# Sparse attention (NSA) on one core: row maxima from a single-pass score matmul, exponentials taken from key-major scores and fed straight to the value product, heads unrolled

## The reference

```python
def masked_softmax(s, mask):
    s = jnp.where(mask, s, -jnp.inf)
    m = jnp.max(s, axis=-1, keepdims=True)
    m = jnp.where(jnp.isfinite(m), m, 0.0)
    p = jnp.exp(s - m)
    return p / jnp.maximum(jnp.sum(p, axis=-1, keepdims=True), 1e-30)

# per block of 128 queries, in nsa_mixer
sc = jnp.einsum('bkgqd,bkcd->bkgqc', qn, k_cmp).astype(jnp.float32) * scale
p_cmp = masked_softmax(sc, cmp_end[None, :] <= t[:, None])
o_cmp = jnp.einsum('bkgqc,bkcd->bkgqd', p_cmp.astype(v_cmp.dtype), v_cmp)
...
ss = jnp.einsum('bkgqd,bkqnd->bkgqn', qr, ks).astype(jnp.float32) * scale
p_s = masked_softmax(ss, (kpos <= t[:, None])[:, :, None])
o_slc = jnp.einsum('bkgqn,bkqnd->bkgqd', p_s.astype(vs.dtype), vs)
...
sw = jnp.einsum('bkgqd,bknd->bkgqn', qr, kw).astype(jnp.float32) * scale
p_w = masked_softmax(sw, wband & (start - SLIDE_WINDOW + ki >= 0))
o_win = jnp.einsum('bkgqn,bknd->bkgqd', p_w.astype(vw.dtype), vw)
o = gb[0][..., None] * o_cmp + gb[1][..., None] * o_slc + gb[2][..., None] * o_win
```

## Time and profile before

| | us |
|---|---|
| median of 3 runs | 4932.07 |
| lowest, highest | 4921.65, 4937.89 |
| the profiled execution, its own time | 4938.08 |
| its span | 4936.3 |
| first to last matmul of this stage | 369.2 (2173.2 to 2542.4) |

### The profile page before, as it was taken

The page is one execution under the profiler, slowest core; times in us unless marked ns, Lnnn a source line. Parts: engine busy times, 40 slices in busy tenths (PEclk is TensorE's granted clock), DMA queues, the critical chain, the costliest instruction groups (busy, mean ns, idle before and its releaser), DMA issues. The chain is left out here.

```text
span 4936.3 us, 63184 instructions
## 1 busy us (share of the span) xinstructions
PE 4619.3 (94%) x21804; PEld 3854.2 (78%) x21804; DVE 2554.3 (52%) x4786; ACT 1741.3 (35%) x2558; POOL 283.3 (6%) x390
## 2 busy tenths in 40 slices
PE   7999989988999899979899999479999999999999
PEld 6887777777888788778788887168888888888887
DVE  6534655654652663355543325859965542344444
ACT  2222233343222322234443223423366662322222
POOL 1100000000100010011100000000000000011010
PEclk9999999999999899965579999789999999999999
DMA  6522201202542453210012221023344444555553
GB/s 234 216 100 100 93 27 47 85 26 77 213 161 86 153 209 127 81 38 1 1 52 86 96 100 69 9 74 115 124 171 175 178 185 176 183 194 193 191 195 141
DMA packets 105432, 589.79 MB, mean 119 GB/s; under 512 B 11778, under 2 KB 12992, under 8 KB 59712
## 3 DMA queue, kind: packets, MB, share of 16 engines
q1 hardware_dynamic: 52800, 369.76, 21.0%
q0 software_dynamic: 52480, 218.13, 12.0%
HBM read 513.36 MB, written 74.48 MB: 119 GB/s over the span
## 5 line engine op out<-in xcount | busy, mean ns | idle before, releaser
L112 DVE TENSOR_TENSOR w_lo<-raw,w_hi 128x2048 fp32r<-128x2048 f32 x331 | 758.7, 2292 | 1160.3 <-ACT w_hi L104 1150.9
L124 PE MATMUL ps<-x_hi,w_hi 128*128 128x512 f32 x2896 | 1150.6, 397 | 43.1 <-DVE x_lo L364 19.8
L125 PE MATMUL ps<-x_lo,w_hi 128*128 128x512 f32 x2896 | 1136.8, 393 | 0.0
L126 PE MATMUL ps<-x_hi,w_lo 128*128 128x512 f32 x2896 | 1136.4, 392 | 0.0
L104 ACT ACTIVATE w_hi<-raw 128x2048 fp32r<-128x2048 f32 x331 | 632.6, 1911 | 815.1 <-PE ps L126 439.0
L124 PEld LDWEIGHTS ps<-x_hi,w_hi 128*128 128x128 f32 x2896 | 549.7, 190 | 162.2 <-issue 44.3
L126 PEld LDWEIGHTS ps<-x_hi,w_lo 128*128 128x128 f32 x2896 | 548.7, 189 | 116.1
L125 PEld LDWEIGHTS ps<-x_lo,w_hi 128*128 128x128 f32 x2896 | 549.9, 190 | 109.8
L2041 PE MATMUL ps<-w_hi,px_gh 128*128 128x512 f32 x1024 | 399.0, 390 | 0.0
L2041 PE MATMUL ps<-w_hi,px_gl 128*128 128x512 f32 x1024 | 399.0, 390 | 0.0
L2041 PE MATMUL ps<-w_lo,px_gh 128*128 128x512 f32 x1024 | 399.0, 390 | 0.0
(11 more groups left out here) (345 smaller groups left out, 6132.3 us busy)
## 6 DMA issues: line engine op xcount, KB each, us to landing
raw<-in_slabs SPq DMA_DIRECT2D x331, 1024.0 KB, 4.8
ada_ring<-in_w_ada POOLq DMA_DIRECT2D x160, 512.0 KB, 4.8
act_dram<-px_act POOLq DMA_DIRECT2D x64, 512.0 KB, 2.9
gate_dram<-ps_g POOLq DMA_DIRECT2D x16, 2048.0 KB, 7.3
px_g<-gate_dram POOLq DMA_DIRECT2D x32, 1024.0 KB, 7.8
px_ai<-act_dram POOLq DMA_DIRECT2D x64, 512.0 KB, 4.7
h_dram<-h SPq DMA_DIRECT2D x2, 2048.0 KB, 8.4
h<-h_dram SPq DMA_DIRECT2D x2, 2048.0 KB, 8.0
```

The source lines that it names most:

```text
L112: nc.vector.tensor_tensor(k.wlo[:, c % 2, :], k.raw[:, c % 2, :], k.whi[:, c % 2, :].bitcast(F32), ALU.subtract).then_inc(k.raw_free, 1)
L124: mm(out, hi, rhs_hi, start=start, stop=False)
L125: mm(out, hi, rhs_lo, start=False, stop=False)
L126: return mm(out, lo, rhs_hi, start=False, stop=stop)
```

## The change

The stage is written anew and its loop is unrolled over 16 heads. A head now has nine items `j`: 0 is the compressed branch, 1 to 4 and 5 to 8 are the selected and the window branch.

- **By query** (`by_query`, for the maxima only): the scores are computed query by row as before, but with the high part of the keys alone, one matmul instead of two. DVE masks and takes the maximum; what it writes besides (`na_junk`) is thrown away. One DVE instruction per head clamps and negates the 12 maxima of each query (`na_nm`).
- **Rows** (`rows`): four small transposes per head turn the negated maxima into three rows of 512 (`na_mrow`), copied from PSUM by ACT.
- **By key** (`by_key`): the scores are computed a second time, key by row, with keys as the stationary operand and up to 512 query columns moving, both parts. Into the same PSUM bank go a matmul of three rows (`na_pick` by `na_mrow`), which subtracts the maxima, and one with the identity and the diagonal mask (`na_diag`), or for the compressed branch one of 31 rows with its mask (`na_cmpT`).
- ACT takes the exponential straight from PSUM into `na_pt`, which is the stationary operand of the value product. The transposes of the probabilities, their copies, the bias and the row sums go away. The values get a column of ones (`na_vo`, `na_vco`, 65 columns), so that the row sum comes out of the value product.
- **Output**: once per head instead of once per block, 12 sums and 768 products at a time; two pairs of banks take turns.
- By query runs two heads ahead of the rest: for heads 0 and 1 it stands before everything else, and the last two heads have none beside them. Staging by GpSimd waits for the last by-key item of the head four before.

The core of the diff:

```diff
+            def by_query(h, j):
+                u = 9 * h + j
+                if j == 0:
+                    pe.wait_ge(s["staged"], h + 1)
+                if u > 1:
+                    pe.wait_ge(s["maxed"], u - 1)
...
+                    last = nc.tensor.matmul(bank(k, u % 2, n), qs[:, h % 4, 1, b * P:(b + 1) * P], kk[:, 0, at:at + n],
+                                            start=True, stop=True)
+            def by_key(h, j):
+                q = item(h, j)
+                pe.wait_ge(s["act"], max(q - 1, row_item(h) + 1))
+                if j == 0:
+                    out = k.ps[0:NC, (2 + q % 2) * T:(3 + q % 2) * T]
+                    nc.tensor.matmul(out, ident[0:NC, 0:NC], cmp_t[:], start=True, stop=False)
+                    for part in range(2):
+                        nc.tensor.matmul(out, kc[:, part, 32 * kv_of(h):32 * kv_of(h) + NC], qs[:, h % 4, 0, :],
+                                         start=False, stop=False)
+                    last = nc.tensor.matmul(out, pick[:, 0, 0:NC], mrow[:, h % 2, :], start=False, stop=True)
+                else:
...
+                    for part in range(2):
+                        nc.tensor.matmul(bank(k, 2 + q % 2, n), kk[:, part, at:at + P], qs[:, h % 4, 1, kb * P:T],
+                                         start=part == 0, stop=False)
+                    nc.tensor.matmul(bank(k, 2 + q % 2, n), pick[:, 1 + (j - 1) // 4, :], mrow[:, h % 2, kb * P:T],
+                                     start=False, stop=False)
+                    last = nc.tensor.matmul(bank(k, 2 + q % 2, P), ident[:], diag[:], start=False, stop=True)
...
-                scores(0)
-                scores(1)
-                for u in range(U):
-                    if u < U - 2:
-                        scores(u + 2)
-                    transposes(u)
-                    if u > 0:
-                        values(u - 1)
-                values(U - 1)
+            for h in range(2):
+                for j in range(9):
+                    by_query(h, j)
+            rows(0)
+            pe.wait_ge(s["consts"], 1)
+            pe.wait_ge(s["vo"], 1)
+            by_key(0, 0)
+            for h in range(NH):
+                for j in range(9):
+                    if j == 2 and h < NH - 1:
+                        rows(h + 1)
+                    if j < 8:
+                        by_key(h, j + 1)
+                    elif h < NH - 1:
+                        by_key(h + 1, 0)
+                    if h < NH - 2:
+                        by_query(h + 2, j)
+                    values(h, j)
```

More of the change, by code:

```diff
@@ L1249, in stage_attend_nsa @@
     nc = k.nc
-    NC, U = 31, 4 * NB * 3
+    NC, W = 31, HD + 1
     with ExitStack() as ctx:
@@ L1275, in blocks, with kv_of, keys_at, item @@
-        def blocks(n):
-            return [(j * P, min(P, n - j * P)) for j in range((n + P - 1) // P)]
+        def kv_of(h):
+            return h // 8
+        def keys_at(h, j):
+            return (2 * ((j - 1) // 4) + kv_of(h)) * T, (j - 1) % 4
+        def item(h, j):
+            return 1 + 10 * h + j + (j > 2 and h < NH - 1)
+        def row_item(h):
+            return 10 * h - 6 if h else 0
+        def out_at(h, b, i):
+            return bank(k, 4 + 2 * (h % 2) + b // 2, W, (3 * (b % 2) + i) * W)
@@ L1278, in _ @@
         @blk.sync
         def _(sp):
-            sp.dma_start(causal[:], d["mask_causal"]).then_inc(s["const"], 16)
-            sp.dma_start(mcmp[:], d["mask_cmp"]).then_inc(s["const"], 16)
+            for dst, src in ((causal[:], "mask_causal"), (mcmp[:], "mask_cmp"), (raw_diag, "mask_diagT"), (raw_cmp, "mask_cmpT")):
+                sp.dma_start(dst, d[src]).then_inc(s["const"], 16)
         @blk.gpsimd
         def _(gp):
[L1285 to L1295, removed]
@@ new lines, in values @@
+            def values(h, j):
+                pe.wait_ge(s["act"], item(h, j) + 1)
+                slot = (9 * h + j) % 3
+                if j == 0:
+                    if h > 1:
+                        pe.wait_ge(s["free"], h - 1)
+                    for b in range(NB):
+                        last = nc.tensor.matmul(out_at(h, b, 0), pt[0:NC, slot, b * P:(b + 1) * P], vco[:, kv_of(h), :],
+                                                start=b % 2 == 0, stop=False)
+                else:
+                    kb, i = (j - 1) % 4, (j - 1) // 4
+                    for b in range(kb, NB):
+                        last = nc.tensor.matmul(out_at(h, b, 1 + i), pt[:, slot, (b - kb) * P:(b - kb + 1) * P],
+                                                vo[:, i, kb, kv_of(h), :], start=False, stop=i == 1 and kb == b and b % 2 == 1)
+                last.then_inc(s["pv"], 1)
@@ L1352, in _ @@
                 rows = slice(HD * half, HD * half + HD)
-                nc.scalar.activation(kc[rows, 0, :], kcp[:].rearrange("p v n -> p (v n)"), ACT.Copy)
-                last = nc.scalar.activation(kk[rows, 0, :], kT[:].rearrange("p b v t -> p (b v t)"), ACT.Copy)
+                A(kc[rows, 0, :], kcp[:].rearrange("p v n -> p (v n)"), ACT.Copy)
+                last = A(kk[rows, 0, :], kT[:].rearrange("p b v t -> p (b v t)"), ACT.Copy)
             last.then_inc(s["khi"], 1)
[L1356 to L1377, removed]
+            A(ident[:], k.ident[:], ACT.Copy)
+            for i in range(3):
+                A(pick[:, i, :], k.ident[0:3, i:i + 1].to_broadcast([3, P]), ACT.Copy)
+            act.wait_ge(s["const"], 64)
+            A(diag[:], raw_diag, ACT.Copy)
+            A(cmp_t[:], raw_cmp, ACT.Copy).then_inc(s["consts"], 1)
+            row_copy(0)
+            for h in range(NH):
+                for j in range(9):
+                    exps(h, j)
+                    if j == 2 and h < NH - 1:
+                        row_copy(h + 1)
         @blk.vector
@@ L1436, in stage_nsa @@
+            ve.wait_ge(s["const"], 64)
+            for h in range(2):
+                for j in range(9):
+                    maxima(h, j)
+                negative(h)
+            for h in range(NH):
+                for j in range(9):
+                    if j == 4 and h > 0:
+                        output(h - 1)
+                    if h < NH - 2:
+                        maxima(h + 2, j)
+                if h < NH - 2:
+                    negative(h + 2)
+            output(NH - 1)
 def stage_nsa(k, d, norm, gate):
```

198 lines of the change are left out of this document (113 added, 85 removed).

## The result

The changed kernel takes **5054.3 us** (median of 4 runs, 5047.7 to 5057.4). The kernel before, run beside it, took 4927.9 us. The ratio is 1.0253 with a 95% interval of 1.0231 to 1.0275: **2.5% slower**. The forecast was 4837 us; the time is that of rival 1, 5047 us, and lies above the range. The span of the profiled execution is 5050.3 us, 114.0 more than the 4936.3 of before. From first to last matmul the stage takes 484.8 us instead of 369.2, which is 115.6 more, so all of the loss is in the stage.

What follows compares the result with a forecast made beforehand. The stage was taken as PE-bound; at high clock 12 + 1.6 + 16 + 261 = 291 us instead of 369, 78 less, or 114 without three-row excursions; 95 was taken, giving 4837 us, eight-in-ten range 4808 to 5045.

Steps and rivals of the forecast that it cites:

- rival 1: By-key items of each head: the clock never holds, PE pays 29.8 us a head, 5047 us in all; chance 0.24.
- what a head costs at the low level: PE's matmuls, row-count switches and type changes per head in the new stage: 29.8 us at the low clock.
- Nine three-row tiles: Selecting and compressed matmuls of each head: each priced like a 31-row tile, 0.38 us low, 0.25 us high.
- The check against the kernel before: Old stage, per head: the same matmul prices sum to 23.0 us at the low level, trace 23.1.
- that case: Whole stage at high clock with three-row tiles costing nothing extra: 114 us less, 4818 us.
- Does the clock rise?: Step on the stage's clock: dense 512-column stretches and removed idle causes favour a rise; high nearly throughout, chance 0.52.
- The sign that the prediction named for being wrong: Stage clock: the prediction is wrong if the clock falls without an idle stretch.
- the fork: Stage at either clock: a head takes 16.5 us high or 29.8 us low, against 23.1 before.
- All the gain hangs on the clock: Stage: at equal clock PE's work is 29% longer, so only a high clock, 16.5 us a head, gains.
- The lead of by query: Stage start: by query of heads 0 and 1 stands alone in front, +12 us.
- The start at the low level: First heads of the stage: some 1.2 heads run low until the clock rises, +16 us.
- rival 3: Between heads: DVE's output or GpSimd's hold stops PE 1 to 2 us a head, 4861 us; chance 0.04.

Runs made afterwards that it cites:

- experiment 1: Changed kernel with na_pick and na_mrow widened from 3 to 128 partitions, zeros in the added rows; 4800.5 us, ratio 0.9723.
- experiment 2: Changed kernel with the selecting matmul and also the compressed branch's mask, values and probabilities padded to 128 rows; 4785.4 us, ratio 0.9694.
- experiment 5: Kernel before with its loop of four rounds unrolled and nothing else changed; 4905.3 us, ratio 0.9957.
- experiment 6: Kernel before, loop unrolled and the compressed values padded from 31 to 128 rows; 4848.6 us, ratio 0.9846.
- experiment 3: Changed kernel with 24 extra unread matmuls of 512 columns right before the first by-key item; 5054.0 us in one run.
- experiment 9: Changed kernel with the selecting matmul at 128 rows and before each a matmul of 31 rows and 32 columns adding zero; 5031.0 us in one run.

## Why the prediction was wrong

**Right: what bounds the stage, and what a head costs at the low level.** PE was forecast at 29.8 us a head and took 29.87; the stage was worked out at 484 us for rival 1 and took 484.8.

**Two terms in this sum were off and cancelled.** Nine three-row tiles were put at the price of the 31-row one, 9 x 0.38 = 3.4 us. They cost 29.87 - 25.13 = 4.7, 0.53 each, inside the bounds that were set (nothing to the double). An item of 512 columns pays 0.13 + 0.30 + 0.16 = 0.59 (distances 1.13, 0.72, 0.27 against 1.00, 0.42, 0.11), one of 128 columns pays 0.13 + 0.19 + 0.06 = 0.38, by these starts of the changed kernel and of the one with 65 rows:

```profile
2353.26 0.67 PE L1355 MATMUL ps<-na_q,na_k 128*128 128x128 f32 x2
2353.86 0.47 PE L1357 MATMUL ps<-na_mrow,na_pick 3*128 3x128 f32 x1
2354.26 0.47 PE L1359 MATMUL ps<-na_diag,na_ident 128*128 128x128 f32 x1
2354.53 0.63 PE L1326 MATMUL ps<-na_k,na_q 128*128 128x384 f32 x1
```
```profile
2317.14 0.67 PE L1355 MATMUL ps<-na_q,na_k 128*128 128x128 f32 x2
2317.61 0.41 PE L1357 MATMUL ps<-na_mrow,na_pick 65*128 65x128 f32 x1
2317.82 0.41 PE L1359 MATMUL ps<-na_diag,na_ident 128*128 128x128 f32 x1
2318.03 0.63 PE L1326 MATMUL ps<-na_k,na_q 128*128 128x384 f32 x1
```

Items of 256 and 384 columns pay 0.58 and 0.59 in the same way. The price of the earlier trace rows came from short matmuls. The rest of the head was forecast at 29.8 - 3.4 = 26.4 and took 25.1. A short matmul behind a long one does not cost the floor of 0.21 but 0.11 (2320.59 to 2320.70), since its load ran under the long one; six of the eight diagonal matmuls of a head stand like this, which is 0.6 of the 1.3. The first values behind a long by-query matmul are short of the floor too (two in 0.28, 2321.23 to 2321.51 with 65 rows); the remainder was not parted. The check against the kernel before did not show this, because it left out the term for changes of type that the sum of the changed kernel has: with 0.14 for each of its 12 groups of scores it would have given 24.7 instead of 23.0, against 23.1. That 5047 came so near to 5054 is partly luck for this reason.

**Nearly right, though never seen in the changed kernel: the high level.** Without the three-row tiles 14.2 us were forecast for a head, and experiment 1 has 13.86; its 4800.5 us stand against the 4818 given for that case. The price of such a tile was put at 0.25 and was too low. Four narrow ones make the head 0.99 longer, but by then the wait of 0.27 is gone. By the starts, an item of 512 columns with three rows takes 0.63 + 0.43 + 0.16 = 1.22 in the kernel with the wide items at three rows, where experiment 1 has 0.55 + 0.23 + 0.06 = 0.84 (2302.72 to 2303.56), so 0.38:

```profile
2267.64 0.70 PE L1355 MATMUL ps<-na_q,na_k 128*128 128x512 f32 x2
2268.27 0.50 PE L1358 MATMUL ps<-na_mrow,na_pick 3*128 3x512 f32 x1
2268.70 0.33 PE L1360 MATMUL ps<-na_diag,na_ident 128*128 128x128 f32 x1
2268.86 0.44 PE L1326 MATMUL ps<-na_k,na_q 128*128 128x512 f32 x1
```

With 128 columns it is 0.29 (0.77 from 2302.13 to 2302.90 with three rows for the narrow items, against 0.48 from 2300.10 to 2300.58 in experiment 1). The nine together would make 13.86 - 0.27 + 7 x 0.38 + 2 x 0.29 = 16.8 us, an estimate that takes the compressed item's tile as a wide one, against 16.5.

**Wrong: the step "Does the clock rise?"** It weighed the stretches of 512 columns and the disappearance of the loop's end and of the hold on DVE for the rise, against pauses which "thin out just these dense stretches", and gave 0.52 to a clock that stays high and 0.24 to one that never does. It never rose: 0.50 over 484.9 us. What it took for the reason of the low level, "many short matmuls behind full weight loads, not because PE waits", was wrong: experiments 1 and 2 have the same short matmuls behind the same loads, and run high from the first head. The falls of before were put down to PE's idle stretches of 1.85 and 7.0 us. Experiment 5 takes the loop's end away and gets 21 us and the same mean clock of 0.58; experiment 6 pads one operand and gets 0.77. The four 31-row tiles a head, whose pauses had been measured in the earlier trace rows, had held the clock of before down too, in part. The change took the places with such tiles from four a head to eleven, most of them with 256 to 512 columns. The sign that the prediction named for being wrong, a clock that falls without an idle stretch, is what experiment 3 shows.

**Right: the fork, and the place that rival 1 named.** It put the loss into the by-key items, where "each dense stretch is cut by two pauses of 0.19"; experiment 9 bears out that such pauses are enough. "All the gain hangs on the clock" stood: in experiment 1 and the changed kernel, which differ in the rows of one operand pair, 13.9 against 29.9 us a head decides between 4800 and 5054 us. The condition that was named (granted clock near 1.0 or 0.5 throughout) tells it at once. Only the chances were put the wrong way round, and the range ended just short of the rival.

**The small terms.** The lead of by query was put at 12 us; the first by-key matmul came 14.1 us after the stage's first (2175.45 to 2189.57). The start at the low level was put at 1.2 heads; where the clock does rise (experiment 1), it does so about 4 us after the first by-key matmul. DVE takes 7.0 us a head (112.35 / 16) where 8 were forecast, ACT 4.8 where at most 6; the two long instructions of the output 0.96 and 1.04 where 0.96 stood. In the changed kernel nothing that counts waits for either, and PE is busy 30.00 of 30 us. At the high level rival 3 has a small part: PE is busy 29.77 of 30 us in experiment 1, by its wait for the maxima of 0.27 us a head, where the rival had 1 to 2.

**What stays open.** Pauses with a 31-row tile of 32 columns bring the level down (experiment 9), and 65 rows without the pauses leave it unsteady. How much each has in the changed kernel can't be parted: each tile of 3, 31 or 64 rows that was run brings both. The kernels with 64 rows and with three differ by some 20 us (5034 against 5054) outside the stage, whose lengths agree (485.0 and 484.8), so that nothing is read from differences of that size between single runs.

## What to carry to other kernels

Before adding a small matmul that selects, broadcasts or masks through a few partitions, pad its contraction to 128 rows with zeros: the columns cost the same here, and it was worth 254 of 5054 us. When a profile shows PE fully busy at the low level, look for weight tiles of few rows (3 to 64 in these runs) between full ones, in the distances of starts and in the loads that begin with their own matmul, before looking for idle time. And if a forecast hangs on the clock, what to ask is which tiles of the new sequence kept the clock down in the old one.

## What the runs showed of the hardware

- A matmul over 3 or 64 rows between full-height ones costs, over its columns, 0.38 us at the low level with 128 columns and 0.59 with 512; over 3 rows at the high level it costs 0.29 and 0.38. Tiles of 31 rows among short matmuls cost 0.38 and 0.26. Over 65 rows the cost is nothing.
- PE can be busy for 481 of 485 us and be granted 0.50 throughout. Even after a burst had lifted it, the level fell with PE fully busy.
- The same sequence of 1600 matmuls ran its stage in 485, 313, 233 and 227 us, with 3, 65 and 128 rows for the selecting matmul and with every tile at 128 rows.
- Four three-row tiles a head of 128 and 256 columns left the clock at 0.96, four of 384 and 512 columns at 0.58.
